# A second gate row computed inside the last attention unit, in the score banks, and another order of modulation sums and merges

## The reference, cut to what matters

```python
rx, rgx, qx, kx, vx, gax, gbx = split_cols(hx @ w_in[l])
y_rx = rglru_output(hf_x, hb_x, rgx, x.dtype)
y_ax = windowed_attention(q_lat, k_lat, v_lat, kc_h, vc_h, sink_logit[l]).astype(x.dtype)
# merge_branches
y = sigmoid(gax) * (y_rx @ w_o_rnn) + sigmoid(gbx) * (y_ax @ w_o_attn)
x = x + g1 * (y @ w_out)
# modulation: sh1, sc1, g1, sh2, sc2, g2 = split(silu(c) @ w_mod + b_mod)
```

## Time and profile before

| What | Value |
|---|---|
| Time, median of 3 runs | 1767.47 us (1767.22 to 1767.74) |
| Profiled execution | 1773.98 us, of it 1772.2 us span |
| PE busy | 1735.1 us, 98% of the span |
| DVE busy | 1206.5 us, 68% |
| ACT busy | 775.8 us, 44% |
| POOL busy | 538.8 us, 30% |
| Mean granted TensorE clock | 0.997 of full speed |
| PE's share of the chain that ended last | 80% |

### The profile page before, as it was taken

One profiled execution on the slowest core, in us unless ns is written; L12 is line 12 of the kernel. 1 busy time (PEld: TensorE's weight loads), 2 busy tenths in 40 slices (PEclk: granted clock), 3 DMA queues, 4 the chain that ended last, 5 costly groups with the idle time before them and its releaser, 6 DMA issues.

```text
span 1772.2 us, 23343 instructions
## 1 busy us (share of the span) xinstructions
PE 1735.1 (98%) x8382; PEld 1438.1 (81%) x8382; DVE 1206.5 (68%) x1386; ACT 775.8 (44%) x1017; POOL 538.8 (30%) x262
## 2 busy tenths in 40 slices
PE   7999999998999999999999999999999999999998
PEld 5897888877888889878888877888888888888887
DVE  7988666777406587867246389999999998424425
ACT  5358778877101188840011145444444444202205
POOL 1036666655245576635457700000000000000000
PEclk9999999999999999999999999999999999999999
DMA  9231111111454300047226412221221224523112
GB/s 369 77 114 39 57 51 51 50 62 43 142 181 118 83 25 0 1 164 257 83 76 230 139 60 95 84 95 71 83 95 71 83 89 161 202 99 133 54 36 95
DMA packets 56149, 177.98 MB, mean 100 GB/s; under 512 B 11794, under 2 KB 12178, under 8 KB 55444
## 3 DMA queue, kind: packets, MB, share of 16 engines
q1 hardware_dynamic: 46964, 148.27, 23.9%
q10 hardware_dynamic: 9120, 28.84, 4.9%
HBM read 140.39 MB, written 31.46 MB: 97 GB/s over the span
## 4 chain that ended last, share of the span: by engine, by line
PE 80%; DVE 7%; issue 2%; ACT 2%; POOL 1%; DMA 1%; SPq 0%; ACTq 0%; DVEq 0%; POOLq 0%
PE acc L919 17%; PE acc L921 17%; PE acc L920 17%; PE gp L919 8%; PE gp L920 8%; PE gp L921 8%; PE acc L1244 2%; PE gp L1069 1%; DMA wst<-in_w_in 1%; DVE y_lo L2356 1%; DVE T_lo L2657 0%; PE gp L1219 0%; PE gp L1218 0%; PE gp L1217 0%; DVE prob L2405 0%
## 5 line engine op out<-in xcount | busy, mean ns | idle before, releaser
L919 PE MATMUL acc<-hx_hi,whi_both 128*128 128x512 f32 x672 | 264.4, 393 | 3.6 <-ACT sg L1477 1.6
L920 PE MATMUL acc<-hx_lo,whi_both 128*128 128x512 f32 x672 | 261.8, 390 | 0.0
L921 PE MATMUL acc<-hx_hi,wlo_both 128*128 128x512 f32 x672 | 261.5, 389 | 0.0
L731 POOL TENSOR_TENSOR whi_both<-wst,ones 128x1024 fp32r<-128x1024 f32 x56 | 149.9, 2677 | 254.5 <-PE acc L921 240.8
L733 POOL TENSOR_TENSOR wlo_both<-wst,whi_both 128x1024 fp32r<-128x1024 f32 x56 | 171.4, 3061 | 4.4
L919 PEld LDWEIGHTS acc<-hx_hi,whi_both 128*128 128x128 f32 x672 | 126.1, 188 | 35.9 <-issue 4.8
L921 PEld LDWEIGHTS acc<-hx_hi,wlo_both 128*128 128x128 f32 x672 | 126.1, 188 | 26.6
L920 PEld LDWEIGHTS acc<-hx_lo,whi_both 128*128 128x128 f32 x672 | 126.2, 188 | 25.1
L1477 ACT ACTIVATE dn_hi<-wst 128x768 fp32r<-128x768 f32 x32 | 27.0, 845 | 182.6 <-PE acc L921 120.7
L919 PE MATMUL acc<-T_hi,fac_hi 128*128 128x512 f32 x264 | 102.8, 389 | 0.4 <-DVE fac_lo L2696 0.4
L921 PE MATMUL acc<-T_hi,fac_lo 128*128 128x512 f32 x264 | 102.7, 389 | 0.0
(11 more groups left out here) (403 smaller groups left out, 4640.5 us busy)
## 6 DMA issues: line engine op xcount, KB each, us to landing
wst<-in_w_in SPq DMA_DIRECT2D x43, 512.0 KB, 3.5
wst<-in_w_up SPq DMA_DIRECT2D x26, 512.0 KB, 4.2
wg<-in_mod_rest ACTq DMA_DIRECT2D x24, 512.0 KB, 5.3
ffn_row_scratch<-ca SPq DMA_DIRECT2D x24, 512.0 KB, 2.6
wst<-in_w_down SPq DMA_DIRECT2D x32, 384.0 KB, 3.2
g_in<-ffn_row_scratch SPq DMA_DIRECT2D x24, 512.0 KB, 7.0
wup<-in_w_up SPq DMA_DIRECT2D x22, 512.0 KB, 4.1
wmod<-in_mod_first SPq DMA_DIRECT2D x16, 512.0 KB, 15.4
```

The costliest lines, as they stand in the source:

```text
L731: nc.gpsimd.tensor_tensor(whi[s][:, 0:kc, :], wst[s][:, 0:kc, :], ones_of(kc), mult).then_inc(S["w_hi"], 1)
L919: mm(out_ap, w_h, x_h, start=first, stop=False)
L920: mm(out_ap, w_h, x_l, start=False, stop=False)
L921: return mm(out_ap, w_l, x_h, start=False, stop=last)
```

## The change

PE computes the second gate row inside the last attention unit, in pieces between its transposes and products, into the first two banks of `gp` (those of score heads 0 and 2, free once DVE has read head 2: `s_neg` at 4u + 3). The gate row behind the attention is gone; the first attention row follows at once. ACT no longer reads `acc[0]` for that gate; it counts `acc_read[0]` by hand once the attention is read out, and has a `second_merge_gate` of its own that reads `gp` and counts `sg_again`. DVE's merge 1 waits for that count. The orders written out by hand become: DVE 3 sums, merge 0, 9 sums, merge 1, 7 sums, merge 2, 5 sums, merge 3; ACT 3 loads, the two sigmoids, 7 loads, gate 2, 7 loads, gate 3, 7 loads.

```diff
+            def second_row(h, ks):
+                for k in ks:
+                    last = three(gp[:, HALF * h:HALF * (h + 1)], whi[(W_S4 + 1) % 2][:, k, :], wlo[(W_S4 + 1) % 2][:, k, :],
+                                 hx_hi[:, k, HALF * h:HALF * (h + 1)], hx_lo[:, k, HALF * h:HALF * (h + 1)], k == 0, k == KC - 1)
+                return last
+
+            def last_unit(n, kh, u):
+                weights(W_S4 + 1)
+                pe.wait_ge(S["s_neg"], 4 * u + 3)
+                second_row(0, range(2))
+                for j in range(3):
+                    flip(n, kh, u, j)
+                second_row(0, range(2, 4))
+                flip(n, kh, u, 3)
+                weigh(n, kh, u, [0])
+                weigh(n, kh, u, [1, 2])
+                second_row(0, range(4, 5))
+                weigh(n, kh, u, [3])
+                second_row(0, range(5, KC))
+                second_row(1, range(KC)).then_inc(S["acc_full"], 1)
...
-            units(pe, attention, lambda n, kh, u: ([flip(n, kh, u, j) for j in range(3)], flip_and_weigh(n, kh, u)))
+            units(pe, attention, last_unit)
             pe.wait_ge(S["o_read"], N_KV * XT)
-            product(A_S4 + 1, W_S4 + 1, hx_hi, hx_lo)
             product(A_S4 + 2, W_S4 + 2, y_hi, y_lo, paced="z_lo_s")
...
+            def second_merge_gate():
+                full(act, A_S4 + 1)
+                act.wait_ge(S["row_silu"], 1)
+                act_of(sg[1][:, :], gp[:, 0:SEQ], ACT.Sigmoid).then_inc(S["sg_again"], 1)
...
             act.wait_ge(S["o_read"], N_KV * XT)
+            act.sem_inc(acc_read[(A_S4 + 1) % 2], 1)
...
             row_again(0)
-            for j in range(3, 6):
-                load_g1(j)
             act.wait_ge(sg_loaded[0], 16 * KC // 2)
             act_of(sg[0][:, :], sg[0][:, :], ACT.Sigmoid).then_inc(S["sg_again"], 1)
-            merge_gate(1, 1, (S["row_silu"], 1))
-            for j in range(6, 14):
+            second_merge_gate()
+            for j in range(3, 10):
                 load_g1(j)
             merge_gate(2, 0, (S["merged"], 1))
-            for j in range(14, 22):
+            for j in range(10, 17):
                 load_g1(j)
             merge_gate(3, 1, (S["merged"], 2))
-            for j in range(22, EARLY_SUMS):
+            for j in range(17, EARLY_SUMS):
                 load_g1(j)
...
-                if isinstance(m, int) and m == 0:
-                    dve.wait_ge(S["sg_again"], AT["sg_again"] + 1)
+                if isinstance(m, int) and m < 2:
+                    dve.wait_ge(S["sg_again"], AT["sg_again"] + m + 1)
...
-            for j in range(6):
+            for j in range(3):
                 add_g1(j)
             merge(0, 0)
-            for j in range(6, 14):
+            for j in range(3, 12):
                 add_g1(j)
             rest_bias(0, 1)
             merge(1, 1)
-            for j in range(14, 22):
+            for j in range(12, 19):
                 add_g1(j)
             merge(2, 0, 1)
-            for j in range(22, EARLY_SUMS):
+            for j in range(19, EARLY_SUMS):
                 add_g1(j)
             merge(3, 1, 1)
```

## The result

| | before | after |
|---|---|---|
| Median of the runs | 1767.74 us (1767.22 to 1769.48, 7 runs) | 1776.03 us (1767.97 to 1778.08, 7 runs) |
| Ratio after / before | | 1.0037, 95% interval 1.0028 to 1.0046 |
| Span of the profiled execution | 1772.2 us | 1766.2 us |

Slower, where 1767.3 was forecast and 1770.5 was the end of the range. Two things have to be read together. The runs of the changed kernel fall in two groups: one at 1767.97, six between 1774.66 and 1778.08. And its profile comes from the one execution at 1768, while the profile of before is 6 us over that kernel's median. So the page of after, against the page of before, looks like a gain, and the trace that tells why the kernel is slower is not this one. First comes what that execution has, then (in the experiments) one of the upper group.

What follows compares the result with a forecast made beforehand. PE, busy 98% of the span, was taken as the bound. Its 5.6 us of losses were nearly all offset by new waits and a clock fall, leaving -0.2 us: 1767.47 - 0.2 = 1767.3 us, range 1762.0 to 1770.5.

Steps and rivals of the forecast that it cites:

- PE's walk to the first attention row: PE's starts followed from 758.33 through the last attention unit: gate row full at 774.1, before at 777.84.
- POOL comes into `y_lo` by turns: POOL's earlier split alternates with DVE's y_lo slices: last slice at 782.4, 4.7 us later, PE waiting 0.8 and 2.8.
- The first rival: y_lo's slices don't give way to POOL, PE never waits there: 1762.0 to 1763 us, chance 0.17.
- the fallen clock: PE's clock falls once behind the new y_lo waits, costing 1.7 us; given 2 in 3.
- 9 x 2.51: Time of DVE's nine sums ahead of merge 1, at 2.51 us each, ending merge 1's first operation at 823.6.
- the second rival: The sums hold PE at merge 1, decided from 2.5 us a sum; at 2.9 PE waits 3.6, 1771.2 us, chance 0.10.
- 9 x 3.2: Upper bound for the nine sums, each held as long as a turn allows: 6 us later.
- the start of that chain: DVE's sums start behind the last y_lo, 5.3 us later than before; crow product at 787.75, taking 1.2.
- the second loss: Last unit's sixteen transposes and what follows run at half clock from about 760, losing PE about 1.7 us.
- the 5.6: Sum in us of PE's four losses between the end of unit 15's products and the third gate row, 0.3%.

Runs made afterwards that it cites:

- The late split: Changed kernel with POOL splitting the third gate row's weights only after all eight y_lo slices; 1764.34 us (ratio 0.9975), repeated at 1762.86 us (0.9968).
- the first trace: The profiled execution of the changed kernel in its first set of seven runs, without a further edit; 1767.97 us.
- a: The changed kernel without an edit, first of three more executions made to catch a slow one with its trace; 1777.92 us.
- e2: Kernel before with the new order of modulation sums and merges alone, second gate row still behind the attention; 1765.89 us, ratio 0.9985.
- e7: Changed kernel with POOL's split held until y_lo is done and the old order of sums and merges (6, 8, 8, 2); 1773.5 us, ratio 1.003.

## Why the prediction was wrong

**Right: PE's walk to the first attention row.** Forecast 14.3 us behind the transposes (774.1 against 759.78), measured 14.1. The last unit's pieces left no hole, and the clock stayed at 1.00 beside them. The page's rule on transposes (the Trainium skill, "TensorE: Matmul & The Clock Gate", "Part 4: PE-mode transpose"), by which the clock might have fallen there, did not show: twelve transposes took 1.50 us.

**Right: POOL comes into `y_lo` by turns.** Forecast 4.7 us more, two waits of 0.8 and 2.8; measured 13.54 against 9.19, 4.4 more, and 0.57 and 2.33. The late split takes all of it away. The Trainium skill, page "SBUF — State Buffer", section "Who interferes with whom", says that an instruction of VectorE with two inputs in SBUF contends with a GpSimd instruction that reads SBUF, and that the lock on the shared port pair is exclusive; POOL's 2.39 alone and 3.34 beside `y_lo` agree. The first rival (no turns) is out, and its price, 5.5 us, is what the late split earned.

**Right, and firmer than I gave it: the fallen clock** behind that wait. I said 2 in 3; it is in all seven traces that have this wait. The third gate row came at 30.1 in five and at 31.1 and 31.2 in two, forecast 28.9 without and 30.6 with the fall. Beyond the waits the row lost 1.7 us in the five, the price that I gave, and 2.7 to 2.8 in the two, where the granted clock was already down to 0.5 when the wait ended. For the lower group the whole sum was near: the fifth gate row was forecast 0.2 us earlier than before, and it came from 0.4 earlier to 0.7 later.

**Wrong: the term "9 x 2.51".** This is the step that failed. I had the mechanism as the second rival, its place (merge 1), its threshold (2.5 us a sum) and that it had no slack, and still gave it 0.10 and 3.6 us. It was the common case: 12 of the 22 timed executions of the changed kernel lie in the upper group, and both that have a trace show it. The nine sums take 21.1 to 21.4 us (2.3 to 2.4 each) when sum 3 is ahead of POOL's split, and 25.6 and 27.9 (2.8 and 3.1 each) when it is behind. My 2.51 was the mean of eight sums in one trace, where the split came 2.4 us behind the first of them (799.50 and 801.91), as if that distance were fixed. The wait, 4.8 to 7.1 us, brings a fall of the clock of its own, 1.9 to 2.8 us on the next row. The bound that I had written, 9 x 3.2, was near the truth, but I let the range end where the rival cost some 3 us. The forecast should have been "63, or 68 to 71 behind T, by a race", with both ends in the range.

**Off in size: the start of that chain.** The DMA of `crow` took 5.7 to 6.8 us in the seven traces with the row in the score banks and the early split, 4.2 in the two with the row behind the attention, and 4.1 to 4.9 with the late split. I had carried 4.16 over, and the 0.7 us between the first trace and a are enough to turn the race of sum 3. Beside it SP now loads the weights that the earlier split has set free. That the two share the DMA engines is what I think; only the times are shown.

**Off in size: the second loss.** The 1.7 us for the clock at 760 are not all there to be won. In e2, whose last unit is that of before, PE waited just as long ahead of the transposes (1.29 us), the clock stayed at 1.00 and twelve of them took 1.50. But the last four then waited 0.54 for `pt_lo`, and the first attention row came at 17.2, not 18.1: the fall had cost 0.9. An execution of before without it has 0.9 us less to win than the 5.6 that I listed; how common that is stays open, with one trace of before.

## What to carry to other kernels

When work of the bottleneck engine moves forward, list what waits for its end: here POOL's split came forward with it, into the one chain that the next row was paced by. Holding that split back by one wait turned a loss of 0.2 to 0.4% into a gain of about 0.3%. And where a bank is released behind a queue of operations whose length depends on turns with another engine, put the release ahead of them, or count each at its longest: a step that has no slack by the sum, in a chain that can only be late, is a loss in part of the executions.

## What the runs showed of the hardware that I had not expected

Which engine gets the turn is a race, and it can be lost several times in a row. In the trace of before POOL's product `si` took 6.24 us at 424.57 while VectorE's three slices of `r_lo` went through without a pause (3.49 us). In the trace of after `si` took 2.83, and it was the same three slices that were held (8.46 us):

```profile
424.57 6.24 POOL L765 TENSOR_TENSOR si<-si,xc 128x1024 f32<-128x1024 f32 x1 [9.75 <-ACT si L1477]
```

```profile
425.05 3.49 DVE L2338 TENSOR_TENSOR r_lo<-Y,r_hi 128x1024 fp32r<-128x1024 f32 x3
```

```profile
422.58 2.83 POOL L765 TENSOR_TENSOR si<-si,xc 128x1024 f32<-128x1024 f32 x1 [9.76 <-ACT si L1497]
```

```profile
423.06 8.46 DVE L2362 TENSOR_TENSOR r_lo<-Y,r_hi 128x1024 fp32r<-128x1024 f32 x3
```

So taking turns one by one, on which the prediction built, is what `y_lo` showed in all seven traces, but it is no law: the trace of before had this counterexample. PE waited 4.3 us for POOL up to 438.7 in the first, and this is most of why that execution was 6 us over its kernel's median; e7 has the same (6.23 and 4.3 us). A small operation pays the full turn: the bias addition of 128x8 took 2.29 us beside POOL, 0.16 alone. And two traces of one kernel can differ by more (10 us here) than the change that they are to explain, so the trace has to be of an execution whose time is that of the group in question.
